# Hybrid attention/mLSTM layer: adaLN modulation by pairs of feature tiles, two last-gate tiles computed at the start, gate columns on head 0's token units

## The chip, the cores and the metric

One core of a Trainium2 chip. The metric is the device time of one execution in microseconds (us), the median of several runs. TensorE multiplies, VectorE (DVE), ScalarE (ACT) and GpSimd (POOL) do the elementwise work, SyncE (SP) and ScalarE issue the DMAs.

## What is computed

One layer on x of 1024 tokens by 1024 features, float32, cut here to what matters:

```python
mod = silu(c) @ w_ada + b_ada
shift, scale, gate = split(mod, 3)
h = rmsnorm(x, norm_w) * (1 + scale) + shift
proj = h @ w_in
aq, ak, av, az, mq, mk, mv, mo, mz, mi, mf, ga, gm = split(proj)
att = sliding_window_attention(rope(aq), rope(ak), av, sinks)   # 16 heads, 4 kv heads, window 128
y_att = (att * silu(az)) @ w_att_branch
hm = mlstm(silu(conv(mq)), silu(conv(mk)), mv, mi + b_i, log_sigmoid(mf + b_f))
y_m = (headnorm(hm) * sigmoid(mo) * silu(mz)) @ w_m_branch
merged = sigmoid(ga) * y_att + sigmoid(gm) * y_m
out = rmsnorm(x + gate * (merged @ w_out), final_norm_w)
```

w_ada has 1024 rows and 3072 columns: shift, scale, gate. w_in has 11,272 columns; mi and mf, the mLSTM's input and forget gates, are 4 columns each; gm, the last gate, is 1024 columns.

## The kernel before, in words

All operands of a large product are split into a high and a low part of 32 bits each (fp32r). A product is three matmuls (`passes`, lines 527 to 529): high x high, low x high, high x low. Features are cut into KT = 8 tiles of 128, tokens into NB = 8 blocks of 128 and two halves of 512.

Weights go through five slots of 128 columns. SP loads a slot (`raw`, 512 KB), POOL splits it with two instructions, w_hi (L482) and w_lo (L484), and TensorE uses it; who reads the last product of a slot frees it (`slot_free`). SP's, POOL's and TensorE's use of the slots is a written order: the tables SLOT_USES and BANK_USES say how often each phase uses a slot and a bank, and every wait is a count worked out from them. POOL takes the splits in program order and waits for a slot even where a later one is ready.

The start: x is loaded (4 MB), squared on ScalarE (L801), its row factors made on POOL (L469, L471), normalised on VectorE (L1040), turned on TensorE (L568) and copied to `xnt` by ScalarE (L806). The small vectors come behind x in SP's queue (L366 to L371). w_ada's shift and scale columns come row tile by row tile, 1 MB each; VectorE adds each, times silu(c), to `mod_acc` (L1083, L1086), and between them makes the rotation angles (L1056 to L1074). TensorE turns the sums (L575), VectorE adds up and makes scale and shift (L1092 to L1098). Then, tile by tile, ScalarE writes h_hi (L815), ScalarE or VectorE x_mod (L817, L1106), VectorE h_lo (L1115). Behind each h_lo, TensorE adds to the gate units: slot 4 holds the 8 columns of mi and mf in 128 mostly empty ones, two units of 512 tokens.

The phases after that: A (four kv heads; per head 8 token units of 384 columns for q, k and v, and 4 feature units for az, with rope, softmax and the attention products beside them; head 0 alone also carries the mLSTM's gate rows, `gate_row_step`), B (the attention branch), C (the mLSTM), D1 (sigmoid of the last gate gm, 8 feature tiles x 2 halves into `sig_m`; beside it ScalarE loads and VectorE sums w_ada's gate columns, L985, L1421), D2 (the mLSTM branch; before it ScalarE writes y_hi, L997, and VectorE y_lo, L1430) and E (w_out, residual, last norm). D1 and D2 use slots 0, 1, 2 and 4 in turn, twice each:

```python
for phase in ("D1", "D2"):
    with pool.Fori(0, 2, 1) as i:
        for s in D_SLOTS:
            split(s, use(phase, s, 0) + i, loads(phase, s, 1) + i)
```

Of the kernel before, what the change touches and what calls it, by code (L numbers as in the profile page):

```python
# [21 lines left out]
F32 = mybir.dt.float32  # L22
# [7 lines left out]
P = 128  # L30
# [30 lines left out]
SLOT_USES = {"G": (0, 0, 0, 0, 1), "A": (4,) * 5, "B": (4, 4, 4, 4, 0), "C": (8,) * 5,  # L61
             "D1": (2, 2, 2, 0, 2), "D2": (2, 2, 2, 0, 2), "E": (1, 1, 1, 1, 0), "E2": (1, 1, 1, 1, 0)}
SLOT_DMAS = {"G": (0, 0, 0, 0, 2), "A": (4, 4, 8, 4, 4), "B": (4, 4, 4, 4, 0), "C": (8,) * 5,
             "D1": (2, 2, 2, 0, 2), "D2": (2, 2, 2, 0, 2), "E": (1, 1, 1, 1, 0), "E2": (1, 1, 1, 1, 0)}
D_SLOTS = (0, 1, 2, 4)
BANK_USES = {"A": 24, "B": 16, "C": 48, "D1": 8, "D2": 8, "E": 8}
# [21 lines left out]
MOD_BY_ACT = (1, 4, 7)  # L88
# [6 lines left out]
def build(nc, x, c, positions, w_ada, b_ada, norm_w, w_in, b_if, att_sinks, conv_q, conv_k,  # L95
          m_norm_w, w_att, w_m, w_out, final_norm_w, inv_freq, out, row_pack, merged_dram):
    with ExitStack() as ctx:
# [29 lines left out]
        bias_if = sb("bias_if", [36, 1])  # L127
        scale1 = sb("scale1", [P, KT])
# [35 lines left out]
        def place(name, shape, dt, offset):  # L164
# [17 lines left out]
        w_mod = place("w_mod", [P, KT, 2 * D], F32, HT)  # L182
# [9 lines left out]
        mod_acc = place("mod_acc", [P, 2 * D], F32, X + 3072)  # L192
# [44 lines left out]
        gate_row = place("gate_row", [P, D], F32, RAW + 3 * 4096)  # L237
# [7 lines left out]
        w2_hi = place("w2_hi", [P, 4, KT, P], F32R, HT)  # L245
        w2_lo = place("w2_lo", [P, 4, KT, P], F32R, HT + 4 * 4096)
# [15 lines left out]
        mod_loaded = [sem(f"mod_loaded{n}") for n in range(KT + 1)]  # L262
# [91 lines left out]
        out_v = out.rearrange("(n p) d -> p n d", p=P)  # L354
        merged_v = merged_dram.rearrange("(k p) t -> p k t", p=P)
# [5 lines left out]
        def _(sp):  # L361
            for n in range(4):
                sp.dma_start(x_in[:, 2 * n:2 * n + 2, :], x_v[:, 2 * n:2 * n + 2, :]).then_inc(x_loaded[n], 16)
            for rows, v, n in ((V_C, c, 8), (V_NW, norm_w, 8), (V_SH, b_ada[0:D], 8), (V_SC, b_ada[D:2 * D], 8),
                               (V_CQ, conv_q, 32), (V_CK, conv_k, 32), (V_MN, m_norm_w, 8)):
                sp.dma_start(vec_rows[rows:rows + n, :], v.rearrange("(r p) -> r p", p=P)).then_inc(vec_loaded, 16)  # L366
            sp.dma_start(pos_i[:, :], positions.rearrange("(n p) -> n p", p=P)).then_inc(small_loaded, 16)
            sp.dma_start(freq[:, :], inv_freq[None, :].broadcast_to([P, HD // 2])).then_inc(small_loaded, 16)
            sp.dma_start(sink[:, :], att_sinks[None, :].broadcast_to([P, 16])).then_inc(small_loaded, 16)
            for q in range(2):  # L370
                sp.dma_start(bias_if[32 * q:32 * q + 4, :], b_if[4 * q:4 * q + 4, None]).then_inc(small_loaded, 16)  # L371

            sp.wait_ge(gate_slot_zeroed, 1)
            sp.dma_start(raw[:, 4, :, 0:4], w_in_v[:, :, MI:MI + 4]).then_inc(slot_loaded[4], 16)
            sp.dma_start(raw[:, 4, :, 32:36], w_in_v[:, :, MF:MF + 4]).then_inc(slot_loaded[4], 16)
            for k in range(KT - 1):
                sp.dma_start(w_mod[:, k, :], w_ada_v[:, k, 0:2 * D]).then_inc(mod_loaded[k], 16)
            for half in range(2):
                t = slice(half * D, (half + 1) * D)
                sp.dma_start(w_mod[:, KT - 1, t], w_ada_v[:, KT - 1, t]).then_inc(mod_loaded[KT - 1 + half], 16)  # L380

            def load(src, s, uses):
                after(sp, slot_split[s], uses)
                sp.dma_start(raw[:, s, :, :], src).then_inc(slot_loaded[s], 16)

            with sp.Fori(0, KVH, 1) as i:
# [6 lines left out]
                sp.dma_start(raw[:, 2, :, 0:HD], src_k).then_inc(slot_loaded[2], 16)  # L393
                sp.dma_start(raw[:, 2, :, HD:P], src_v).then_inc(slot_loaded[2], 16)
# [24 lines left out]
            with sp.Fori(0, 2, 1) as i:  # L419
                for k, s in enumerate(D_SLOTS):  # L420
                    src = w_in_v[:, :, bass.ds(sp.snap(GM + k * P + i * 512), P)]
                    load(src, s, use("D1", s, 0) + i)
# [1092 lines left out]
```

## Time and profile before

| what | value |
|---|---|
| runs | 1435.89, 1434.66, 1434.6 us; median 1434.66 |
| profiled execution, span | 1435.3 us (the listed runs lie around it; nothing else is listed for it) |
| TensorE busy | 1340.0 us (93%), 6846 matmuls |
| VectorE busy | 750.4 us (52%) |
| ScalarE, POOL busy | 396.6 us (28%), 491.6 us (34%) |
| mean DMA rate | 62 GB/s, 89.28 MB |

In the rows further down, PE is TensorE's matmuls, PEld its weight loads, DVE VectorE, ACT ScalarE, POOL GpSimd, SPq SyncE's queue. L527 is line 527 of the kernel. A matmul's duration is longer than the step from one to the next, since they are pipelined. PEclk is the granted clock of TensorE: 1.00 is 2.4 GHz, 0.50 is 1.2 GHz.

### The profile page before, as it was taken

Reading aid. Unit: us, or ns where it says so; the run is one execution under the profiler, and the core shown is the slowest. Engines: PE = TensorE matmul, PEld = TensorE weight load, DVE = VectorE, ACT = ScalarE, POOL = GpSimd, SP = SyncE. Lnnn points to the kernel's source line nnn. Section 1 sums busy time; section 2 is a strip of 40 time slices with the busy share of each in tenths; the row PEclk is TensorE's granted clock in tenths of the full one; section 3 lists DMA queues with packets and bytes.
Section 4 is the critical chain, followed back from the end, with each engine's and each line's share of the span. In section 5 each row is a group of like instructions: output and inputs, shape, how many; then the busy total and the mean of one; then the engine's idle time right before and its main releaser. Section 6 shows DMA issues by size and latency. Waiting matters only on the chain.

```text
span 1435.3 us, 19403 instructions
## 1 busy us (share of the span) xinstructions
PE 1340.0 (93%) x6846; PEld 1138.8 (79%) x6846; DVE 750.4 (52%) x1297; ACT 396.6 (28%) x926; POOL 491.6 (34%) x248
## 2 busy tenths in 40 slices
PE   2399998999989999999999999999999999899998
PEld 2297796978867888877988898889789888788886
DVE  5979888695776000065256426633672421366445
ACT  5342634334342010013221322233223311311111
POOL 4613204132045343273054205412531333335230
PEclk9599999999999999999999999999999999999999
DMA  9501102011021121050041004101310123322502
GB/s 350 137 15 30 45 2 59 15 29 29 0 58 35 54 88 59 15 162 16 1 117 44 0 0 132 29 0 41 91 44 15 44 74 98 107 76 68 193 16 103
DMA packets 119830, 89.28 MB, mean 62 GB/s; under 512 B 13305, under 2 KB 111721, under 8 KB 118894
## 3 DMA queue, kind: packets, MB, share of 16 engines
q1 hardware_dynamic: 116288, 76.16, 17.8%
q10 hardware_dynamic: 3502, 12.61, 2.5%
q8 instruction: 23, 0.38, 0.1%
q14 instruction: 17, 0.14, 0.0%
HBM read 80.35 MB, written 8.41 MB: 62 GB/s over the span
## 4 chain that ended last, share of the span: by engine, by line
PE 78%; DVE 14%; issue 4%; ACT 2%; DMA 1%; POOL 1%; DVEq 0%; ACTq 0%; SPq 0%; POOLq 0%
PE pp L527 22%; PE pp L529 22%; PE pp L528 22%; DVE conv L1382 2%; PE pp L713 2%; PE pp L723 2%; PE pp L633 1%; DVE prob L1232 1%; DVE y_lo L1289 1%; PE pp L624 1%; PE pp L602 1%; PE pp L616 1%; PE pp L705 1%; PE pp L617 1%; PE pp L718 1%
## 5 line engine op out<-in xcount | busy, mean ns | idle before, releaser
L482 POOL TENSOR_TENSOR w_hi<-raw,ones 128x1024 fp32r<-128x1024 f32 x101 | 201.4, 1994 | 828.6 <-ACTq L346 492.0
L527 PE MATMUL pp<-h_hi,w_hi 128*128 128x512 f32 x912 | 363.1, 398 | 14.8 <-DVE h_lo L1115 9.5
L528 PE MATMUL pp<-h_lo,w_hi 128*128 128x512 f32 x912 | 357.6, 392 | 0.0
L529 PE MATMUL pp<-h_hi,w_lo 128*128 128x512 f32 x912 | 357.1, 392 | 0.0
L484 POOL TENSOR_TENSOR w_lo<-raw,w_hi 128x1024 fp32r<-128x1024 f32 x101 | 257.2, 2546 | 7.9
L527 PEld LDWEIGHTS pp<-h_hi,w_hi 128*128 128x128 f32 x912 | 172.9, 190 | 52.6 <-issue 10.3
L529 PEld LDWEIGHTS pp<-h_hi,w_lo 128*128 128x128 f32 x912 | 172.6, 189 | 36.7
L528 PEld LDWEIGHTS pp<-h_lo,w_hi 128*128 128x128 f32 x912 | 172.9, 190 | 35.2
L527 PE MATMUL pp<-w_hi,h_hi 128*128 128x384 f32 (+1 forms) x512 | 162.1, 317 | 0.6 <-DVE roped L1209 0.6
L529 PE MATMUL pp<-w_hi,h_lo 128*128 128x384 f32 (+1 forms) x512 | 158.2, 309 | 0.0
L528 PE MATMUL pp<-w_lo,h_hi 128*128 128x384 f32 (+1 forms) x512 | 158.0, 309 | 0.0
L527 PE MATMUL pp<-y_hi,w_hi 128*128 128x512 f32 x256 | 101.7, 397 | 6.5 <-DVE y_lo L1430 4.2
L529 PE MATMUL pp<-y_hi,w_lo 128*128 128x512 f32 x256 | 101.2, 395 | 0.0
L528 PE MATMUL pp<-y_lo,w_hi 128*128 128x512 f32 x256 | 101.1, 395 | 0.0
L527 PEld LDWEIGHTS pp<-w_hi,h_hi 128*128 128x128 f32 x512 | 96.9, 189 | 3.2 <-issue 1.2
L528 PEld LDWEIGHTS pp<-w_lo,h_hi 128*128 128x128 f32 x512 | 97.0, 189 | 1.0
L529 PEld LDWEIGHTS pp<-w_hi,h_lo 128*128 128x128 f32 x512 | 96.9, 189 | 0.0
L1310 DVE TENSOR_TENSOR mix_a<-sig_a,pp 128x512 f32<-128x512 f32 x16 | 11.0, 687 | 144.3 <-PE pp L529 144.0
L1326 DVE SCALAR_TENSOR_TENSOR s_dec<-pp,dec 128x128 f32<-128x128 f32 x32 | 9.3, 292 | 136.3 <-PE pp L705 124.7
L527 PEld LDWEIGHTS pp<-y_hi,w_hi 128*128 128x128 f32 x256 | 48.9, 191 | 18.7 <-issue 3.2
L528 PEld LDWEIGHTS pp<-y_lo,w_hi 128*128 128x128 f32 x256 | 49.1, 192 | 10.2
L529 PEld LDWEIGHTS pp<-y_hi,w_lo 128*128 128x128 f32 x256 | 49.0, 191 | 10.3
(216 smaller groups left out, 1947.6 us busy)
## 6 DMA issues: line engine op xcount, KB each, us to landing
raw<-w_in SPq DMA_DIRECT2D x72, 512.0 KB, 3.8
w_mod<-w_ada SPq DMA_DIRECT2D x7, 1024.0 KB, 11.1
x_in<-x SPq DMA_DIRECT2D x4, 1024.0 KB, 8.2
raw<-w_att SPq DMA_DIRECT2D x8, 512.0 KB, 5.1
merged_dram<-mix_a ACTq DMA_DIRECT2D x8, 512.0 KB, 2.6
w_gate<-w_ada ACTq DMA_DIRECT2D x8, 512.0 KB, 3.5
raw<-w_m SPq DMA_DIRECT2D x8, 512.0 KB, 3.7
mix_in<-merged_dram ACTq DMA_DIRECT2D x8, 512.0 KB, 3.3
```

The lines of the kernel that those rows point to most:

```text
L482: pool.tensor_tensor(hi, raw[:, s, :, :], one, ALU.mult).then_inc(slot_hi[s], 1)
L484: pool.tensor_tensor(lo, raw[:, s, :, :], hi.bitcast(F32), ALU.subtract).then_inc(slot_split[s], 1)
L527: pe.matmul(o, lh, rh, start=first, stop=False)
L528: pe.matmul(o, lh, rl, start=False, stop=False)
L529: return pe.matmul(o, ll, rh, start=False, stop=last)
L602: ins = pe.matmul(bank(2)[:, g * P:(g + 1) * P], q_parts[:, m % 2, g, :, :], ident_r[:, :], start=True, stop=True)
L616: pe.matmul(o, q, k_hi[:, keys], start=True, stop=False)
L617: ins = pe.matmul(o, q, k_lo[:, keys], start=False, stop=True)
L624: ins = pe.transpose(bank(5)[:, g * P:(g + 1) * P], prob[:, g, :], ident[:, :])
L713: ins = pe.matmul(bank(4)[:, 0:MV], mq_t[:, f, n * P:(n + 1) * P], state[:, f, :], start=(f == 0), stop=(f == 1))
L723: ins = pe.matmul(bank(6 + f)[:, 0:MV], k_w[:, n % 2, f * P:(f + 1) * P], v_aug[:, n % 2, :], start=True, stop=True)
L1382: dve.scalar_tensor_tensor(out=conv[:, :], in0=xpad[:, j:j + S], scalar=taps[:, j, n // 2:n // 2 + 1], in1=conv[:, :], op0=ALU.mult, op1=A ...
```

## The change

Four things change together.

1. **w_ada by pairs of feature tiles.** SP loads it in four pairs (2 MB each: 256 shift and 256 scale columns, all 1024 rows, in rows of 1 KB). Of a pair's 8 row tiles VectorE sums 4 (pair 0) or 6 (pairs 1 to 3) into `mod_acc`, TensorE takes the other 4 or 2 as one-column matmuls straight from w_mod and adds VectorE's sum by a matmul with ones (`mod_sums`). Scale and shift of a pair are ready by themselves, and h follows by pairs. The rotation angles come after the last h_lo.
2. **Two of the eight tiles of D1 at the start.** w_in's columns of gm tiles 0 and 1 are loaded first of all into slots 3 and 4 and split by ScalarE and VectorE. Behind each h_lo, TensorE runs 12 matmuls: two tiles, two halves, three passes. ScalarE takes the sigmoids, stores them to DRAM (`early_dram`) and loads them back before D1. D1 has six tiles left.
3. **Gate columns on head 0.** The weight store is laid out as 8 + 5 x 128 columns per row tile, and the 8 columns of mi and mf stand ahead of slot 0, so that head 0's token units take 392 columns instead of 384. VectorE copies the 8 columns of each block to `g_tok`; TensorE turns them at the start of head 1, and they go through DRAM (`gate_dram`) to rows. `gate_row_step` runs in head 1.
4. The small loads are issued by ScalarE; POOL makes the row factors of x by twos.

The diff, cut to its core:

```diff
-SLOT_USES = {"G": (0, 0, 0, 0, 1), "A": (4,) * 5, "B": (4, 4, 4, 4, 0), "C": (8,) * 5,
-             "D1": (2, 2, 2, 0, 2), "D2": (2, 2, 2, 0, 2), "E": (1, 1, 1, 1, 0), "E2": (1, 1, 1, 1, 0)}
+SLOT_USES = {"G": (0, 0, 0, 1, 1), "A": (4,) * 5, "B": (4, 4, 4, 4, 0), "C": (8,) * 5,
+             "D1": (2, 2, 1, 0, 1), "D2": (2, 2, 2, 0, 2), "E": (1, 1, 1, 1, 0), "E2": (1, 1, 1, 1, 0)}
+EARLY = 2
+D1_TILES = [(tile, D_SLOTS[n % 4], n // 4) for n, tile in enumerate(range(EARLY, KT))]
+GATE_LOADS = (2, 2, 1, 1, 1, 1)
+PAIRS = KT // 2
+J_PE = (4, 2, 2, 2)
+SUMS_BEFORE = (0, 0, 2, 4)
+WCOLS = G8 + 5 * P
...
         def _(sp):
+            for n in range(EARLY):
+                sp.dma_start(raw[:, :, cols_of(3 + n)], w_in_v[:, :, GM + n * P:GM + (n + 1) * P]).then_inc(slot_loaded[3 + n], 16)
...
-            for k in range(KT - 1):
-                sp.dma_start(w_mod[:, k, :], w_ada_v[:, k, 0:2 * D]).then_inc(mod_loaded[k], 16)
+            for p in range(PAIRS):
+                for half in range(2):
+                    src = w_ada_v[:, :, half * D + 2 * P * p:half * D + 2 * P * (p + 1)]
+                    sp.dma_start(w_mod[:, half, p, :, :], src).then_inc(mod_loaded[p], 16)
+            sp.dma_start(raw[:, :, 0:G8], w_in_v[:, :, MI:MI + G8]).then_inc(g8_loaded, 16)
...
-            for phase in ("D1", "D2"):
-                with pool.Fori(0, 2, 1) as i:
-                    for s in D_SLOTS:
-                        split(s, use(phase, s, 0) + i, loads(phase, s, 1) + i)
+            for _, s, n in D1_TILES:
+                split(s, use("D1", s, n), loads("D1", s, n + 1))
+            with pool.Fori(0, 2, 1) as i:
+                for s in D_SLOTS:
+                    split(s, use("D2", s, 0) + i, loads("D2", s, 1) + i)
...
+            def mod_sums(p):
+                pe.wait_ge(mod_loaded[p], 32)
...
+                for j in range(KT - J_PE[p], KT):
+                    for half in range(2):
+                        for kk in range(2):
+                            pe.matmul(bank((0, 6)[half] + kk)[:, p:p + 1], w_mod[:, half, p, j, kk * P:(kk + 1) * P], silu_c[:, j:j + 1],
+                                      start=(j == KT - J_PE[p]), stop=False)
+                pe.wait_ge(mod_summed, sum(KT - J_PE[m] for m in range(p + 1)))
...
             pe.wait_ge(x_evac, 16)
...
             for k in range(KT):
+                for p in range(PAIRS):
+                    if SUMS_BEFORE[p] == k:
+                        mod_sums(p)
                 pe.wait_ge(h_lo_ready, k + 1)
...
+                for n in range(2 * EARLY):
+                    s, half = 3 + n // 2, n % 2
...
         def _(act):
+            for s in (3, 4):
+                act.wait_ge(slot_loaded[s], 16)
+                act.activation(w_hi[:, :, cols_of(s)], raw[:, :, cols_of(s)], ACT.Copy).then_inc(slot_hi[s], 1)
+            act.wait_ge(vecs_ready, 1)
+            act.activation(silu_c[:, :], vecs[:, V_C:V_C + KT], ACT.Silu).then_inc(silu_c_ready, 1)
...
         def _(dve):
+            mod_products(0)
+            mod_scale(0)
+            mod_products(1)
+            split_h(0)
+            mod_scale(1)
+            split_h(1)
+            mod_products(2)
+            split_h(2)
+            mod_scale(2)
+            split_h(3)
+            mod_products(3)
+            split_h(4)
+            mod_scale(3)
+            for k in range(5, KT):
+                split_h(k)
...
             attend(0)
-            with dve.Fori(0, KVH - 1, 1) as i:
+            attend(1, 0, gate_rows=True)
+            with dve.Fori(1, KVH - 1, 1) as i:
                 attend(i + 1, i)
```

How instructions move, at three places.

VectorE at the start, from the first sum over w_ada on, before (a part; `mod_acc` is the running sum, `ang` and `turns` the angles):

```order
L1083 TENSOR_SCALAR mod_acc<-w_mod,silu_c 128x2048 [waits mod_loaded0,silu_c_ready,angle_step]
L1056 TENSOR_TENSOR ang<-pos_col,freq 128x256
L1086 SCALAR_TENSOR_TENSOR mod_acc<-w_mod,silu_c,mod_acc 128x2048 [waits mod_summed,mod_loaded1]
L1060 TENSOR_SCALAR turns<-ang 128x256 [waits angle_step]
L1086 SCALAR_TENSOR_TENSOR mod_acc<-w_mod,silu_c,mod_acc 128x2048 [waits mod_summed,mod_loaded2]
```

and now:

```order
L1168 TENSOR_SCALAR mod_acc<-w_mod,silu_c 128x512 [waits silu_c_ready,mod_loaded0]
L1171 SCALAR_TENSOR_TENSOR mod_acc<-w_mod,silu_c,mod_acc 128x512 [waits mod_summed] x3
L1179 TENSOR_TENSOR scale_t<-pp,sc_bias 128x2 [waits vecs_ready,mod_full]
L1180 TENSOR_TENSOR shift<-pp,vecs 128x2
L1182 TENSOR_TENSOR scale<-scale_t,vecs 128x2 [waits mod_step]
L1168 TENSOR_SCALAR mod_acc<-w_mod,silu_c 128x512 [waits silu_c_ready,mod_loaded1]
L1171 SCALAR_TENSOR_TENSOR mod_acc<-w_mod,silu_c,mod_acc 128x512 [waits mod_summed] x5
L1196 TENSOR_TENSOR h_lo<-x_mod,h_hi 128x1024 [waits h_hi_ready,x_mod_act]
```

The sums are short and dependent, each pair's scale stands behind its own sum, and the angles are gone from between them.

ScalarE at its beginning, before:

```order
L801 ACT_TABLE_LOAD
L801 ACTIVATE pp,x_ssq<-x_in 128x1024 [waits x_loaded0]
L801 ACTIVATE pp,x_ssq<-x_in 128x1024 [waits x_squared,x_loaded0]
```

and now:

```order
L840 DMA pos_i<-positions 8x128
L841 DMA freq<-inv_freq 128x32
L842 DMA sink<-att_sinks 128x16
L844 DMA bias_if<-b_if 4x1 x2
L848 ACT_TABLE_LOAD
L848 ACTIVATE w_hi<-raw 128x8x128 [waits slot_loaded3]
L848 ACTIVATE w_hi<-raw 128x8x128 [waits slot_loaded4]
L850 ACT_TABLE_LOAD
L850 ACTIVATE silu_c<-vecs 128x8 [waits vecs_ready]
L857 ACTIVATE pp,x_ssq<-x_in 128x1024 [waits x_loaded0]
```

The loads, the two splits and silu now stand ahead of the squares.

POOL at the end of D1 and the beginning of D2, before (the body of the loop over D2, behind the same body for D1, which ends with slot 4):

```order
L481 REGISTER_ALU [waits slot_free0]
L482 TENSOR_TENSOR w_hi<-raw,ones 128x1024 [waits slot_loaded0]
L112 REGISTER_ALU
L484 TENSOR_TENSOR w_lo<-raw,w_hi 128x1024 [waits slot_hi0]
L482 TENSOR_TENSOR w_hi<-raw,ones 128x1024 [waits slot_loaded1,slot_free1]
L484 TENSOR_TENSOR w_lo<-raw,w_hi 128x1024 [waits slot_hi1]
L481 ISA [waits slot_free2]
L482 TENSOR_TENSOR w_hi<-raw,ones 128x1024 [waits slot_loaded2]
```

and now the last four rows of D1, which ends with slots 0 and 1 (slot 4 stands just ahead of them), and the first of D2's loop:

```order
L496 TENSOR_TENSOR w_hi<-raw,ones 128x8x128 [waits slot_loaded0,slot_free0]
L498 TENSOR_TENSOR w_lo<-raw,w_hi 128x8x128 [waits slot_hi0]
L496 TENSOR_TENSOR w_hi<-raw,ones 128x8x128 [waits slot_loaded1,slot_free1]
L498 TENSOR_TENSOR w_lo<-raw,w_hi 128x8x128 [waits slot_hi1]
L525 UNCONDITIONAL_BRANCH
L525 ISA
L495 REGISTER_ALU [waits slot_free0]
L496 TENSOR_TENSOR w_hi<-raw,ones 128x8x128 [waits slot_loaded0]
```

D2's slot order is as before, 0, 1, 2, 4, but the tiles of D1 that free them last are now in slots 0 and 1, and were in slots 2 and 4.

## Rows read from the trace of the kernel before

**Rows 1.** The page: the chain that ended last, shares of the span by engine.
```profile
PE 78%; DVE 14%; issue 4%; ACT 2%; DMA 1%; POOL 1%; DVEq 0%; ACTq 0%; SPq 0%; POOLq 0%
```
**Rows 2.** By stretch: length; PE, PEld, DVE, ACT, POOL busy; PEclk; DMA share, GB/s.
```profile
60.00:70.00 10.00, 5.19 (x12) 4.14 (x13) 9.08 (x11) 7.84 (x7) 1.83 (x1) 0.50 0.32 81
```
**Rows 3.** The chain in order of time, start and us: the scale.
```profile
61.96 0.18 DVE scale L1098
```
**Rows 4.** By stretch, stage D1.
```profile
1158.20:1245.30 87.10, 87.10 (x385) 71.82 (x383) 18.60 (x15) 9.59 (x16) 35.44 (x16) 1.00 0.33 97
```
**Rows 5.** Timeline of TensorE (start, us, engine, line): gate units, first of head 0.
```profile
66.22 0.63 PE L527 MATMUL pp<-h_hi,w_hi 128*128 128x512 f32 x1
66.65 0.63 PE L528 MATMUL pp<-h_lo,w_hi 128*128 128x512 f32 x1
...
78.70 0.33 PE L527 MATMUL pp<-w_hi,h_hi 128*128 128x384 f32 x1
78.87 0.34 PE L528 MATMUL pp<-w_lo,h_hi 128*128 128x384 f32 x1
```
**Rows 6.** Timeline, the small loads on SP, and their first reader.
```profile
2.98 0.42 SPq L366 DMA_DIRECT2D vec_rows<-c  x1
...
6.90 0.67 SPq L371 DMA_DIRECT2D bias_if<-b_if  x2
...
15.31 0.41 PE L556 MATMUL pp<-ident,vec_rows 104*128 104x104 f32 x1 [15.31 <-DMA vec_rows<-m_norm_w]
```
**Rows 7.** Timeline of ScalarE at the start: table load, squares, evacuations.
```profile
0.81 1.28 ACT L801 ACT_TABLE_LOAD   x1 [0.81 <-PEq L1485]
...
7.01 1.03 ACT L801 ACTIVATE pp<-x_in 128x1024 f32<-128x1024 f32 x1
...
8.26 1.03 ACT L801 ACTIVATE pp<-x_in 128x1024 f32<-128x1024 f32 x1
...
29.94 6.53 ACT L806 ACTIVATE xnt<-pp 128x512 f32<-128x512 f32 x13 [0.25 <-PE pp L568]
```
**Rows 8.** Timeline 33 to 73 us, VectorE, POOL and TensorE's turns of mod_acc.
```profile
33.04 2.34 DVE L1086 SCALAR_TENSOR_TENSOR mod_acc<-w_mod,silu_c,mod_acc 128x2048 f32<-128x2048 f32 x1
...
38.57 3.96 POOL L482 TENSOR_TENSOR w_hi<-raw,ones 128x1024 fp32r<-128x1024 f32 x1 [12.67 <-DMA raw<-w_in]
...
40.70 3.98 DVE L1086 SCALAR_TENSOR_TENSOR mod_acc<-w_mod,silu_c,mod_acc 128x2048 f32<-128x2048 f32 x1
42.61 4.27 POOL L484 TENSOR_TENSOR w_lo<-raw,w_hi 128x1024 fp32r<-128x1024 f32 x1
...
50.13 1.94 PE L575 MATMUL pp<-ident,mod_acc 128*128 128x128 f32 x8 [14.88 <-DVE mod_acc L1086]
...
71.77 0.81 DVE L1106 TENSOR_SCALAR x_mod<-xnt,scale,shift 128x1024 f32<-128x1024 f32 x1
...
72.49 3.58 DVE L1115 TENSOR_TENSOR h_lo<-x_mod,h_hi 128x1024 fp32r<-128x1024 f32 x3
```
**Rows 9.** Timeline from D1 to D2: POOL, VectorE, TensorE.
```profile
1236.65 2.40 POOL L484 TENSOR_TENSOR w_lo<-raw,w_hi 128x1024 fp32r<-128x1024 f32 x1
1245.55 1.89 POOL L482 TENSOR_TENSOR w_hi<-raw,ones 128x1024 fp32r<-128x1024 f32 x1 [6.50 <-ACTq L346]
1247.52 2.70 POOL L484 TENSOR_TENSOR w_lo<-raw,w_hi 128x1024 fp32r<-128x1024 f32 x1
...
1246.68 12.51 DVE L1430 TENSOR_TENSOR y_lo<-y,y_hi 128x512 fp32r<-128x512 f32 x16 [5.24 <-ACT y_hi L997]
...
1250.82 0.80 PE L527 MATMUL pp<-y_hi,w_hi 128*128 128x512 f32 x1 [1.43 <-DVE y_lo L1430]
```
**Rows 10.** Timeline of VectorE: the first rope product of heads 0, 1 and 2.
```profile
84.81 0.49 DVE L1201 TENSOR_TENSOR rot_c<-pp,cos 128x320 f32<-128x320 f32 x1
...
173.06 0.48 DVE L1201 TENSOR_TENSOR rot_c<-pp,cos 128x320 f32<-128x320 f32 x1
...
260.05 0.48 DVE L1201 TENSOR_TENSOR rot_c<-pp,cos 128x320 f32<-128x320 f32 x1
```

More of the change, by code:

```diff
@@ L417, in _ @@
                         sp.dma_start(dec[:, :], src).then_inc(dec_loaded, 16)
[L419 to L422, printed above, removed]
+            for tile, s, n in D1_TILES:
+                load(w_in_v[:, :, GM + tile * P:GM + (tile + 1) * P], s, use("D1", s, n))
             with sp.Fori(0, 2, 1) as i:
@@ L581, in _ @@
+            pe.wait_ge(x_evac, 16)
             for k in range(KT):
+                for p in range(PAIRS):
+                    if SUMS_BEFORE[p] == k:
+                        mod_sums(p)
                 pe.wait_ge(h_lo_ready, k + 1)
-                for half in range(2):
+                for n in range(2 * EARLY):
+                    s, half = 3 + n // 2, n % 2
+                    if k == 0 and half == 0:
+                        after(pe, slot_split[s], use("G", s, 1))
                     t = slice(half * HALF, (half + 1) * HALF)
-                    ins = passes(bank(6 + half), (w_hi[:, 4, k, :], w_lo[:, 4, k, :]), (h_hi[:, k, t], h_lo[:, k, t]),
-                                 k, k == 0, k == KT - 1)
@@ L587, in _ @@
-            ins.then_inc(gates_full, 1)
+                    ins = passes(bank(2 + n), (w_hi[:, k, cols_of(s)], w_lo[:, k, cols_of(s)]),
+                                 (h_hi[:, k, t], h_lo[:, k, t]), k, k == 0, k == KT - 1)
+                    if k == KT - 1:
+                        ins.then_inc(early_full, 1)
             def turn_k(i, m):
@@ L753, in _ @@
                             ins.then_inc(h_turned, 1)
-            for phase, hi, lo, ready in (("D1", h_hi, h_lo, None), ("D2", y2_hi, y_lo, y2_lo_ready)):
-                with pe.Fori(0, 2, 1) as i:
-                    for k, s in enumerate(D_SLOTS):
-                        after(pe, slot_split[s], use(phase, s, 1) + i)
-                        for half in range(2):
-                            feature_unit(phase, 4, i, 2 * k + half, s, half, hi, lo, ready=ready)
+            for e, (_, s, n) in enumerate(D1_TILES):
+                after(pe, slot_split[s], use("D1", s, n + 1))
+                for half in range(2):
+                    feature_unit("D1", 0, 0, 2 * e + half, s, half, h_hi, h_lo)
+            with pe.Fori(0, 2, 1) as i:
+                for k, s in enumerate(D_SLOTS):
+                    after(pe, slot_split[s], use("D2", s, 1) + i)
+                    for half in range(2):
+                        feature_unit("D2", 4, i, 2 * k + half, s, half, y2_hi, y_lo, ready=y2_lo_ready)
             pe.wait_ge(gate_bias_added, 1)
@@ L773, in _ @@
                         after(pe, slot_split[s], use("E2", s, 1))
-                wh, wl = (w_hi[:, 0:4], w_lo[:, 0:4]) if half == 0 else (w2_hi[:, :], w2_lo[:, :])
                 for n in range(NB):
@@ new lines, in split_h @@
+            def split_h(k):
+                by_act = sum(m in MOD_BY_ACT for m in range(k + 1))
+                if k in MOD_BY_ACT:
+                    dve.wait_ge(x_mod_act, by_act)
+                else:
+                    dve.wait_ge(mod_step, 4 * (k // 2 + 1))
+                    dve.wait_ge(x_evac, 16)
+                    dve.tensor_scalar(x_mod[:, k, :], xnt[:, k, :], scale1[:, k:k + 1], shift[:, k:k + 1],
+                                      ALU.mult, ALU.add).then_inc(x_mod_dve, 1)
+                    dve.wait_ge(x_mod_dve, k + 1 - by_act)
+                dve.wait_ge(h_hi_ready, k + 1)
+                dve.tensor_tensor(h_lo[:, k, :], x_mod[:, k, :], h_hi[:, k, :].bitcast(F32), ALU.subtract).then_inc(h_lo_ready, 1)
```

369 lines of the change are left out of this document (205 added, 164 removed).

## The prediction

> **What bounds the kernel now.** I read first who carries the chain that ended last: TensorE 78% of the span, VectorE 14% [rows 1]. So a microsecond of matmul removed where TensorE runs without a gap is a microsecond gained; work moved to where TensorE waits can be free. The table by stretch shows such a place: from 60 to 70 us TensorE is busy 5.19 of 10 us at a granted clock of 0.50 [rows 2]. The chain says why: the modulation scale is ready at 61.96 us [rows 3], after all 8 MB of w_ada have been summed on VectorE; no matmul with weights can start before. The other end of the change, the last-gate stage D1, is the opposite: 87.10 us without an idle moment, clock 1.00 [rows 4]. Its 384 matmuls (8 tiles x 2 halves x 8 k x 3) give 0.2268 us each.
>
> **Part 1: two of eight D1 tiles go to the start.** D1 loses 96 matmuls x 0.2268 = **-21.8 us**, all on the path [rows 4]. Its weight splits, its eight w_gate loads and sums keep their number; they fit, since VectorE is busy only 18.60 of the 87 us.
>
> **Part 2: the start.** Before, head 0's first matmul is at 78.70 us [rows 5]; I work out when it comes now.
> ScalarE: it now issues the twelve small loads, which took SP 2.98 to 7.57 = 4.6 us [rows 6], so it is free at 5.4. Then a table load 1.28, two copies of 128x1024 at about 1.25, a table load 1.28, silu 0.21: 10.7. Eight squares at a pitch of 1.25: 20.7 [rows 7] (x stands behind 1 MB of w_in now, but is there before ScalarE gets to it). Sixteen evacuations at 0.60 (13 in 6.53 before, less what overlaps; [rows 7]): 30.3.
> TensorE then makes 20 one-column products of w_ada. The nearest row is the eight 128x128 transposes of mod_acc, 1.94 us at half clock, so 0.24 each there and 0.12 at full clock [rows 8]; I take 0.12, as the transposes of x have just ended: 2.4 us. Three tiny vector operations: 0.6. **First scale at 33.4**, against 61.96. The bound above is 0.24, +2.4 us more; below, nothing.
> VectorE from there, in its written order: three times six products of 512 columns. 2048 columns take 2.34, so 512 cost some 0.62, and with the wait for their own result 0.8; the first is a plain multiply, 0.5: 4.5 x 3 = 13.5. Eight h_lo at 1.19 (3 in 3.58) = 9.5, four x_mod at 0.81 = 3.2 [rows 8], three scale triples at 0.6 = 1.8, about 1.5 of waits for TensorE and ScalarE: 29.5, so **62.9** if nothing disturbs it.
> POOL disturbs it. In the same stretch before, VectorE's 2.34 us sum takes 3.98 and POOL's 2.40 us w_lo takes 4.27 [rows 8]: the first ends at 44.68, the second at 46.88, each having waited for the whole instruction of the other. They alternate. The Trainium skill, SBUF — State Buffer, section "Who interferes with whom", calls this an exclusive lock between the two, held for a whole instruction; the trace agrees, with 3.98 for 2.34. Head 0's first slot was split from 38.57 us [rows 8], as soon as it had landed behind w_ada; behind 1 MB more of SP's loads that is some 41 us. Slots 0, 1 and 2 are split then by six POOL instructions, 3 x (1.89 + 2.40) = 12.9 us (durations of [rows 9], before any wait). New is that h_lo and the products lie in just this stretch, with a gap after each in which POOL comes in. Taken in full: last h_lo at **75.8**. Slots 3 and 4 wait for the early units.
> Behind the last h_lo lie twelve matmuls: 2.7 us at full clock, 12 x 0.43 = 5.1 at the low one [rows 5]. I take 4.2: **head 0 starts at 80.0, +1.3**. Its third token unit needs bank 0 back, so the first rope. That now waits for four sigmoids, a store, a table load, sin, and cos on VectorE, while POOL splits slots 3 and 4 (8.6 us): about +1.2 more than the 8 us of two units hide. Together **+2.5**. Bounds: with POOL's 12.9 hidden, -10.5; with the low clock in all 96 early matmuls (41 us behind the first h_lo at 39.5, and the sums) and dear products, +7.
>
> **Part 3: gate columns on head 0.** The 48 gate matmuls at the start are replaced by 8 columns in 192 matmuls. 384 columns step by 0.173 and 512 by 0.2268, so 8 columns cost 3.3 ns: **+0.6** [rows 4, 5].
>
> **Part 4: D1 to D2.** POOL splits slots in the written order. Before, when D1 ended only slot 4 was left: w_hi at 1245.55 and w_lo at 1247.52; the second y_lo, and with it TensorE's second matmul group at 1250.82, waited for that [rows 9]. Now the last tiles use slots 0 and 1, and slots 2 and 4, long free, stand behind slot 1 in POOL's queue. So three splits instead of one fall on the sixteen y_lo (12.51 us, [rows 9]): four more POOL instructions, 2 x 4.3 = 8.6 us, before the sixth y_lo. TensorE had hidden about 2.5 us of y_lo behind its low clock there; it gets that clock for longer and loses it again. **+8**; bounds 0 (VectorE goes first) and +10.
>
> **Part 5: the heads.** Row steps move from head 0 to head 1, and the gate rows go through DRAM. First rope to first rope is 88.25 us in head 0 and 86.99 in head 1 [rows 10], so these steps cost little more than 1.3 where they stand. Eight copies of 8 columns, two more table loads and a DRAM trip in a busier head: **+1**, bounds -2 and +4. The strided layout of w_hi and w_lo I cost at nothing: DMA rows stay 512 bytes, and POOL is idle between splits; if each split took longer, it would show in parts 2 and 4.
>
> **Sum** against the profiled execution's span: 1435.3 - 21.8 + 2.5 + 0.6 + 8 + 1 = 1425.6. The span lies 0.6 above the median of 1434.66, so **1425.0**. Low ends: 1435.3 - 21.8 - 10.5 + 0.6 + 0 - 2 = 1401.6; high ends: 1435.3 - 21.8 + 7 + 0.6 + 10 + 4 = 1435.1.
>
> **Rivals.**
> A. *POOL hardly hurts.* Its instructions fall into VectorE's waits (x_evac, the sums) and VectorE goes first at D2. Then part 2 gives up to -10.5 and part 4 nothing: 1403 to 1414, say **1408**. Against it: in [rows 8] POOL came in after every VectorE operation.
> B. *The low clock.* TensorE waits between its bursts of twelve, and after its wait at the start it worked at the low clock [rows 2, 5]. If each burst runs at 1.2 GHz, the early units end at 83 to 84 and D2 begins slower: **1431**. The Trainium skill, TensorE: Matmul & The Clock Gate, section "HAM oscillation — how this bites in real kernels", holds that bursts broken by waits each start at the low clock, which speaks against feeding TensorE tile by tile; by it the time would be this rival's.
> C. *Gate rows stall head 1.* ScalarE waits for a store and VectorE for two loads, and table loads stand before the softmax; if none of it is covered, two trips of about 3 us and 2 x 1.28 us: **1434**.
> D. *Slower: the vectors land late.* Silu stands ahead of the squares on ScalarE and needs the seventh vector load, which landed at 15.3 us before, behind 4 MB of x [rows 6]. On ScalarE's own queue I expect 6 to 8. If it comes only behind all 13 MB of SP's queue, near 39 us, the squares start 30 us late; POOL's 12.9 are then hidden: +17, **1442**. It starts to cost at 10 us and eats the gain by about 20.
>
> **How the numbers follow.** The sum 0.56; A 0.16; B 0.10, of which 0.04 within 0.2%; C 0.10, of which 0.06 within and 0.04 above; D 0.08. 0.2% is 2.9 us, about what a measurement can tell from no change. Faster 0.56 + 0.16 + 0.06 = 0.78; same 0.10; slower 0.12. The range takes in the sum's bounds, most of A, B and part of C: 1407 to 1434.
>
> **What would show it.** First scale near 33 us; w_hi and w_lo of slots 0 to 2 between the products, each VectorE operation beside them 2 us long; head 0's first matmul near 80; D1 in 65.3 us without a gap; after it six POOL instructions in a row, and y_lo some 20 us long for sixteen. I am wrong if head 0 starts before 72 or after 87, if D1 has gaps, or if y_lo takes 13 us as before.

## The result, and the profile after

The changed kernel takes 1446.90 us (median of 4 runs, 1445.56 to 1448.26) against 1434.63 for the kernel before: ratio 1.0077, 95% interval 1.0064 to 1.0089. It is **slower by 12.3 us**; the forecast was 1425.0, with 1434 as its upper end. The profiled execution took 1445.56 us with a span of 1443.8.

What the forecast named at the start came true within 2 us. The start, in the timelines of TensorE, VectorE and POOL of the changed kernel (start, length, engine, line, output<-inputs):

```profile
28.29 3.76 PE L595 MATMUL pp<-silu_c,w_mod 128*128 128x1 f32 x32 [1.30 <-ACT xnt L860]
...
34.12 0.16 DVE L1182 TENSOR_TENSOR scale<-scale_t,vecs 128x2 f32<-128x2 f32 x1
```
```profile
43.55 12.42 DVE L1171 SCALAR_TENSOR_TENSOR mod_acc<-w_mod,silu_c,mod_acc 128x512 f32<-128x512 f32 x5
55.90 3.36 DVE L1196 TENSOR_TENSOR h_lo<-x_mod,h_hi 128x1024 fp32r<-128x1024 f32 x1
...
74.17 1.22 DVE L1196 TENSOR_TENSOR h_lo<-x_mod,h_hi 128x1024 fp32r<-128x1024 f32 x1
```
```profile
43.39 1.89 POOL L496 TENSOR_TENSOR w_hi<-raw,ones 128x1024 fp32r<-128x1024 f32 x1 [21.91 <-DMA raw<-w_in]
45.36 2.72 POOL L498 TENSOR_TENSOR w_lo<-raw,w_hi 128x1024 fp32r<-128x1024 f32 x1
```

The scale comes at 34.1 (forecast 33.4; [rows 3] had 61.96), in part by luck, as the account of part 2 below shows. POOL's six split instructions, of which two are shown, lie from 43.4 to 58.2, and in that stretch five products that take 3.90 us elsewhere take 12.42. The last h_lo ends at 75.4 (forecast 75.8). Head 0's first matmul comes at 81.78 (forecast 80.0; [rows 5] had 78.70).

The turn from D1 to D2, timelines of POOL and VectorE; it answers to [rows 9]:

```profile
1243.64 1.89 POOL L496 TENSOR_TENSOR w_hi<-raw,ones 128x1024 fp32r<-128x1024 f32 x1 [6.64 <-ACTq L369]
1245.61 2.70 POOL L498 TENSOR_TENSOR w_lo<-raw,w_hi 128x1024 fp32r<-128x1024 f32 x1
1248.27 2.34 POOL L496 TENSOR_TENSOR w_hi<-raw,ones 128x1024 fp32r<-128x1024 f32 x1
...
1255.76 2.68 POOL L498 TENSOR_TENSOR w_lo<-raw,w_hi 128x1024 fp32r<-128x1024 f32 x1
```
```profile
1244.78 20.23 DVE L1535 TENSOR_TENSOR y_lo<-y,y_hi 128x512 fp32r<-128x512 f32 x16 [5.39 <-ACT y_hi L1074]
```

Six POOL instructions in a row, sixteen y_lo in 20.2 us instead of 12.5: as forecast. And the chain is of the same make as in [rows 1]:

```profile
PE 76%; DVE 15%; ACT 4%; issue 4%; DMA 1%; DVEq 0%; SPq 0%; ACTq 0%
```

So the time went elsewhere. I set the same events of the two traces side by side; each line is the length of one stretch:

| stretch | before | after | difference | forecast |
|---|---|---|---|---|
| start to the first rope of head 0 | 84.8 | 90.0 | +5.2 | +2.5 |
| head 0, first rope to first rope | 88.3 | 86.0 | -2.2 | gates +0.6, and the row steps' share of +1 |
| head 1 | 87.0 | 95.1 | +8.1 | the rest of that +1 |
| head 2 | 86.4 | 86.9 | +0.5 | 0 |
| head 3, stages B and C, to the first sigmoid of D1 | 818.3 | 825.8 | **+7.4** | 0 |
| D1, first to last sigmoid | 80.7 | 59.8 | -20.9 | -21.8 |
| last sigmoid of D1 to first merged | 13.6 | 21.3 | +7.7 | +8 |
| D2, E and the stores | 176.2 | 178.9 | **+2.7** | 0 |

Sum +8.5, the difference of the spans. The other 3.8 of the 12.3 lie between executions: every execution that is listed with its span has a time 1.7 to 1.8 above it, so the profiled one of before stands for some 1437.1, 2.4 above the median of its kernel, and the profiled one of the changed kernel lies 1.3 below its median (its four runs are two and two, 1445.6 and 1445.9, 1447.9 and 1448.3; the last section comes back to that).

Two things are large and were not in the sum: head 1, and a slow drift through stages that the diff hardly touches. The drift is in the step from matmul to matmul. Stretches of TensorE in D1, in E's first half and in E's second half (length, busy with count, clock, DMA share, GB/s), kernel before:

```profile
1190.00:1230.00 40.00, 40.00 (x179) 1.00 0.32 95
1375.00:1390.00 15.00, 15.00 (x68) 1.00 0.00 0
1412.00:1427.00 15.00, 15.00 (x68) 1.00 0.25 102
```

The same stretches of the changed kernel:

```profile
1190.00:1230.00 40.00, 40.00 (x175) 1.00 0.40 119
1375.00:1390.00 15.00, 15.00 (x66) 1.00 0.01 2
1412.00:1427.00 15.00, 15.00 (x68) 1.00 0.25 103
```

No idle time and the clock at 2.4 GHz in both, but fewer matmuls in the same 40 us. The start times of the matmuls in D1 give a step of 0.2267 us before and **0.2314** after, and so do all 512-column units of B, C and D2 with w as their weights; 0.2325 in E's first half, where w is the moving operand; and again 0.2267 in E's second half, whose w2 tiles are laid out apart.

### The profile page after: what moved, and what is told of

Read it like the earlier page. It is cut to its first block, busy times and chain, and to the rows that moved or that the text cites. A ratio compares the mean times of both kernels' runs of the same rounds, so it can differ in the third digit from the quotient of the medians.

```text
span 1443.8 us, 19335 instructions
## 1 busy us (share of the span) xinstructions
PE 1365.1 (95%) x6895; PEld 1147.0 (79%) x6895; DVE 756.7 (52%) x1327; ACT 402.2 (28%) x932; POOL 471.3 (33%) x234
## 4 chain that ended last, share of the span: by engine, by line
PE 76%; DVE 15%; ACT 4%; issue 4%; DMA 1%; DVEq 0%; SPq 0%; ACTq 0%
PE pp L541 21%; PE pp L543 21%; PE pp L542 21%; DVE conv L1487 2%; PE pp L752 2%; PE pp L762 2%; DVE prob L1336 2%; PE pp L663 1%; DVE y_lo L1394 1%; PE pp L654 1%; PE pp L744 1%; PE pp L646 1%; DVE mod_acc L1171 1%; PE pp L632 1%; PE pp L647 1%
## 5 line engine op out<-in xcount | busy, mean ns | idle before, releaser
L496 POOL TENSOR_TENSOR w_hi<-raw,ones 128x1024 fp32r<-128x1024 f32 x98 | 194.9, 1989 | 849.6 <-ACTq L369 516.8
L498 POOL TENSOR_TENSOR w_lo<-raw,w_hi 128x1024 fp32r<-128x1024 f32 x98 | 249.3, 2544 | 7.7
L542 PEld LDWEIGHTS pp<-h_lo,w_hi 128*128 128x128 f32 x896 | 170.0, 190 | 38.7
L541 PE MATMUL pp<-w_hi,h_hi 128*128 128x256 f32 (+2 forms) x512 | 163.0, 318 | 1.4 <-DVE roped L1313 1.3
L542 PE MATMUL pp<-w_lo,h_hi 128*128 128x256 f32 (+2 forms) x512 | 158.4, 309 | 0.0
L543 PE MATMUL pp<-w_hi,h_lo 128*128 128x256 f32 (+2 forms) x512 | 158.4, 309 | 0.0
```

The source lines that it names most:

```text
L496: pool.tensor_tensor(hi, raw[:, :, cols_of(s)], one, ALU.mult).then_inc(slot_hi[s], 1)
L498: pool.tensor_tensor(lo, raw[:, :, cols_of(s)], hi.bitcast(F32), ALU.subtract).then_inc(slot_split[s], 1)
L541: pe.matmul(o, lh, rh, start=first, stop=False)
L542: pe.matmul(o, lh, rl, start=False, stop=False)
L543: return pe.matmul(o, ll, rh, start=False, stop=last)
```

## The experiments

### Where a matmul's operand starts

The changed layout puts eight gate columns ahead of the slots in each row of w_hi and w_lo: a slot starts 32 bytes into a row, and rows are 2592 bytes apart, so that seven of the eight rows of a slot start 32 to 224 bytes past a multiple of 256. (Starts are counted from the kernel's base address here and below. The source rounds the base up to a multiple of 64; no run shows where it lies beyond that.) I first took the start alone, in the kernel before:

```diff
-        WHI, WLO = RAW + 5 * 4096, RAW + 10 * 4096
-        YO = WLO + 5 * 4096
+        WHI, WLO = RAW + 5 * 4096 + 32, RAW + 10 * 4096 + 32
+        YO = WLO + 5 * 4096 + 32
```

> The kernel before, with w_hi and w_lo each moved by 32 bytes (and what lies behind them by 64), nothing else. Theory 1: a stationary operand that starts at 32 bytes past a multiple of 64 costs each matmul 4.5 ns (the 512-column pitch of the feature units was 0.2267 us in the kernel before and 0.2312 in the changed one, and stayed 0.2267 in stage E, where w is the moving operand). Then the pitch in D1 becomes 0.2312 here, and 3504 such matmuls give +15.8: about 1450. Theory 2: it is the row pitch of 2592 bytes, or the strided write, or the unrolled code, that costs it: then the pitch stays 0.2267 and the time 1434.7.

Measured: 1453.47 us, ratio 1.0126 (1.0108 to 1.0144), the kernel before on the same chip at 1436.88. D1 shows the fewest matmuls yet:

```profile
1190.00:1230.00 40.00, 40.00 (x173) 1.00 0.32 95
```

The step is 0.2333, and +16.6 us for a shift of 32 bytes (64 for what lies behind w_lo). In D1 the moving operand h has not moved, so the step there is the doing of the weights' start alone: theory 1, though with 6.6 ns and not 4.5, and the row pitch is not needed for it. My aside on stage E in that expectation was wrong: it holds for E's second half only. Here that half steps by 0.2333 too; its weights g_hi have moved by 64 bytes, g_lo and w2 have not.

In the changed kernel, eight more unused columns (G8 = 8 is the number of gate columns):

```diff
+OFF = 2 * G8
-WCOLS = G8 + 5 * P
+WCOLS = OFF + 5 * P
-            return slice(G8 + s * P, G8 + (s + n) * P)
+            return slice(OFF + s * P, OFF + (s + n) * P)
```

> The changed kernel with eight unused columns ahead of the gate columns, so that the slots start at 64 bytes and the row pitch is 2624. Theory 1 (alignment of the stationary operand): the 512-column pitch of the feature units is 0.2267 again, 3456 matmuls x 4.5 ns less: 1446.9 - 15.5 = 1431. Theory 2 (the row pitch or the strided write as such): pitch 0.2312, time 1446.9.

Measured: 1448.84 us, ratio 1.0077 (1.0060 to 1.0095), step 0.2317. **A miss**: rows that start at 64, 128, 192 and 0 bytes past a multiple of 256 in turn gain nothing. That did not clear the alignment, only my 64. Two more shifts of the kernel before:

```diff
-        WHI, WLO = RAW + 5 * 4096, RAW + 10 * 4096
-        YO = WLO + 5 * 4096
+        WHI, WLO = RAW + 5 * 4096 + 128, RAW + 10 * 4096 + 128
+        YO = RAW + 15 * 4096 + 256
```

> The kernel before with w_hi and w_lo each moved by 128 bytes (what lies behind w_lo by 256), nothing else. With 32 bytes the 512-column pitch of every unit with w as stationary operand was 0.2333 us instead of 0.2267. Theory 1 (only multiples of 256 bytes are free of the cost): pitch 0.2333 in D1 again, time + some 14 to 16. Theory 2 (a multiple of 128 is enough): 0.2267, time as before.

Measured: 1453.24 us (2 runs), ratio 1.0117 (1.0088 to 1.0146); step 0.2323 in D1 and where w moves in E's first half, and 0.2267 in E's second half. Theory 1, with a step a little shorter than expected.

```profile
1190.00:1230.00 40.00, 40.00 (x174) 1.00 0.32 92
```

The same with 256 in place of 128 on the first line:

> The kernel before with w_hi and w_lo each moved by 256 bytes. Theory 1 (a multiple of 256 is enough, as for g_hi, which stands at 256 past a multiple of 512 in the changed kernel and steps by 0.2267): pitch 0.2267, time as before. Theory 2 (512 is needed, or the distance between the two operands counts): pitch above 0.2267, time + 10 or more.

Measured: 1437.06 us, ratio 1.0003 (0.9992 to 1.0014), step 0.2267.

```profile
1190.00:1230.00 40.00, 40.00 (x178) 1.00 0.36 105
```

So of the shifts of w tried (32, 128 and 256 bytes) only 256 is free; 64 was seen only mixed with others, in a_off64's rows, and in g_hi. Then the cure in the changed kernel: raw stays as it is, w_hi and w_lo get rows of 704 columns.

```diff
 WCOLS = G8 + 5 * P
+OFF = 64
+WPAD = OFF + 5 * P
-        w_hi = place("w_hi", [P, KT, WCOLS], F32R, WHI)
-        w_lo = place("w_lo", [P, KT, WCOLS], F32R, WLO)
+        w_hi = place("w_hi", [P, KT, WPAD], F32R, WHI)
+        w_lo = place("w_lo", [P, KT, WPAD], F32R, WLO)
```

> The changed kernel with w_hi and w_lo padded to rows of 704 columns, slots from column 64, so that each stationary operand starts at a multiple of 256 bytes; raw keeps its rows of 648. Theory 1 (start of the stationary operand): pitch 0.2267 in all feature units, B, C, D1, D2 give back some 10 to 12: 1435 to 1437. Theory 2 (the row pitch that is no multiple of the slot, or reading and writing with a stride): pitch stays 0.2312, time 1446.9.

Measured: 1437.41 us, ratio **0.9998** (0.9985 to 1.0010): the whole loss is gone. Step 0.2267 throughout:

```profile
1190.00:1230.00 40.00, 40.00 (x178) 1.00 0.35 100
```

Against the table above, head 3 to D1 is +0.3 instead of +7.4, D1 58.4 instead of 59.8, and D2 to the end -0.2 instead of +2.7: 11.4 us of layout. It still reads and writes with a stride that is no multiple of a slot (2816 bytes, a slot being 512) and keeps the odd raw rows, so theory 2 is out. By count it could have been more: 3456 matmuls x 4.7 ns = 16.2. The 1536 of stage C gave back 2.5 of their 7.2 (first to last s_dec 464.1 us before the cure, 461.6 with it); what else bounds that stage was not looked into.

### The turn from D1 to D2

```diff
-D1_TILES = [(tile, D_SLOTS[n % 4], n // 4) for n, tile in enumerate(range(EARLY, KT))]
+D1_TILES = [(2, 0, 0), (3, 1, 0), (4, 2, 0), (5, 4, 0), (6, 2, 1), (7, 4, 1)]
```

(and D1's slot uses and loads (1, 1, 2, 0, 2).)

> The changed kernel with D1's six tiles in slots 0, 1, 2, 4, 2, 4 instead of 0, 1, 2, 4, 0, 1. Theory 1 (POOL's queue at the turn from D1 to D2 costs about 8 us): only slot 4 is left to split when D1 ends, the sixteen y_lo take 12.5 us instead of 20, and the time is 1446.9 - 7.5 = 1439.4. Theory 2 (TensorE's low clock or y_lo itself sets the turn): below 2 us gained, 1445 or above.

Measured: 1441.05 us, ratio 1.0029 (1.0014 to 1.0044), 6 to 7 below the changed kernel. POOL and VectorE there:

```profile
1247.01 1.89 POOL L496 TENSOR_TENSOR w_hi<-raw,ones 128x1024 fp32r<-128x1024 f32 x1 [3.02 <-ACTq L369]
1248.98 2.70 POOL L498 TENSOR_TENSOR w_lo<-raw,w_hi 128x1024 fp32r<-128x1024 f32 x1
```
```profile
1248.07 12.59 DVE L1535 TENSOR_TENSOR y_lo<-y,y_hi 128x512 fp32r<-128x512 f32 x16 [3.00 <-ACT y_hi L1074]
```

One split instead of three, y_lo in 12.6, last sigmoid to first merged 13.7 instead of 21.3. Theory 1: part 4 was right in mechanism and size.

### The gate rows in head 1

ScalarE in head 1 of the changed kernel, and VectorE's fourth and fifth rope there:

```profile
197.60 1.06 ACT L899 ACTIVATE row_e<-row_e 4x1024 f32<-4x1024 f32 x1
198.68 1.28 ACT L901 ACT_TABLE_LOAD   x1
199.97 1.06 ACT L901 ACTIVATE row_e<-row_e 4x1024 f32<-4x1024 f32 x1
201.05 0.60 ACT L924 ACTIVATE q_t<-pp 128x512 fp32r<-128x512 f32 x1
201.55 0.27 ACT L925 ACTIVATE k_hi<-pp 128x128 fp32r<-128x128 f32 x1
201.84 1.28 ACT L931 ACT_TABLE_LOAD   x1
```
```profile
195.42 0.48 DVE L1305 TENSOR_TENSOR rot_c<-pp,cos 128x320 f32<-128x320 f32 x1
...
201.85 0.29 DVE L1326 TENSOR_TENSOR k_lo<-pp,k_hi 128x128 fp32r<-128x128 f32 x1 [2.96 <-ACT k_hi L925]
...
206.10 0.48 DVE L1305 TENSOR_TENSOR rot_c<-pp,cos 128x320 f32<-128x320 f32 x1
```

Exp, a table load, Ln and the table load back are 4.7 us, and the softmax of the block stands behind them: 10.7 us from rope to rope, 6.5 in the kernel before. Before, these two stood in step 0 of head 0, where no softmax runs yet. Moved to where ScalarE waited 11.4 us:

```diff
-                if n == 4:
-                    act.wait_ge(row_step, 5)
...
                     if 4 <= u <= NB + 3:
                         exponentials(i, u - 4)
+                    if gate_rows and u == 8:
+                        act.wait_ge(row_step, 5)
...
```

> The changed kernel with ScalarE's Exp and Ln of the gate rows in head 1 moved from the end of step 4 to step 8, where ScalarE waited 11.4 us for the last rope. Theory 1 (these two and the two table loads around them, 4.7 us, stand in the path of the softmax): the fifth rope of head 1 comes 6.5 us after the fourth instead of 10.7, and the time is about 4 us less, 1443. Theory 2 (head 1 is limited by VectorE, which has the row steps on top): 1446 to 1447, the 4 us come back by the eighth rope.

Measured: 1441.12 us, ratio 1.0035 (1.0021 to 1.0048). Fourth to fifth rope is 6.5 again:

```profile
195.99 0.48 DVE L1304 TENSOR_TENSOR rot_c<-pp,cos 128x320 f32<-128x320 f32 x1
...
202.47 0.48 DVE L1304 TENSOR_TENSOR rot_c<-pp,cos 128x320 f32<-128x320 f32 x1
```

Head 1 takes 90.1 us instead of 95.1. Theory 1, a little stronger than expected. The 3 us still above the other heads stand beside the row steps that VectorE has on top there; they were not taken apart.

### All three

> The changed kernel with the 256-byte rows, D1 in slots 0, 1, 2, 4, 2, 4, and Exp and Ln of the gate rows at step 8 of head 1. If the three costs are separate places of one path, the gains add: 1446.9 - 11 - 6 - 5 = 1425, below the kernel before by 10. If one is hidden behind another, 1428 to 1435.

Measured: **1423.76 us**, ratio 0.9914 (0.9891 to 0.9936), the kernel before at 1437.03. From the changed kernel's 1.0077 that is -0.0163; the three single ratios give -0.0079, -0.0048 and -0.0042, together -0.0169. Within these intervals they add, as three places on one path would.

### The start

POOL held back until h_lo is made:

```diff
+            pool.wait_ge(h_lo_ready, KT)
             with pool.Fori(0, KVH, 1) as i:
                 for s in range(5):
```

> The kernel of a_three, with POOL's first split held back until all eight h_lo are made. Theory 1 (my step in part 2: six POOL instructions take 12.9 us out of VectorE's row of products and h_lo): the last h_lo ends near 63 us instead of 77, slots 0 to 2 are split from then on and head 0's first matmul comes near 77 instead of 83, 4 to 6 us less: 1418 to 1420. Theory 2 (POOL's work falls into waits of VectorE that are there anyway): the last h_lo comes at most 3 us earlier and head 0 starts 10 us later: 1433.

Measured: 1421.93 us, ratio 0.9903 (0.9886 to 0.9919). The last h_lo starts at 64.8 instead of 74.5:

```profile
54.64 3.90 DVE L1179 SCALAR_TENSOR_TENSOR mod_acc<-w_mod,silu_c,mod_acc 128x512 f32<-128x512 f32 x5
...
64.81 1.23 DVE L1204 TENSOR_TENSOR h_lo<-x_mod,h_hi 128x1024 fp32r<-128x1024 f32 x1
```

POOL's 12.9 us did cost VectorE 9.7. But head 0 starts at 79.8 instead of 82.0, the first rope comes at 89.0 instead of 90.3, and by head 1 nothing is left (175.4 against 175.0). The mechanism is theory 1's; the gain is neither theory's, and within the interval it is none. TensorE is through with the early units at 72.5 there and stands idle until head 0, which needs slots 0 to 2; the last of POOL's six split instructions for them, now behind the h_lo, ends at 79.6:

```profile
79.79 0.66 PE L549 MATMUL pp<-w_hi,h_hi 128*128 128x392 f32 x1 [7.26 <-issue]
```

So the splits hold head 0 back there. The Trainium skill, SBUF — State Buffer, section "Who interferes with whom", says that VectorE and GpSimd hold their shared port pair exclusively; the trace agrees, with the same five products at 12.42 us beside POOL and 3.90 without.

A second candidate for what ate the rest: sin and cos. In the changed kernel they come late, and cos runs beside POOL's split of slot 4 (85.12 to 89.53):

```profile
83.13 1.28 ACT L882 ACT_TABLE_LOAD   x1 [0.47 <-ACT sig_early L878]
84.43 0.42 ACT L882 ACTIVATE sin<-ang 128x256 f32<-128x256 f32 x1
```
```profile
85.26 2.04 DVE L1221 TENSOR_TENSOR turns<-turns 128x256 f32<-128x256 f32 x1 [6.03 <-ACT turns L883]
87.33 2.36 DVE L1223 TENSOR_SCALAR cos<-turns 128x256 f32<-128x256 f32 x1
...
90.01 0.48 DVE L1305 TENSOR_TENSOR rot_c<-pp,cos 128x320 f32<-128x320 f32 x1
```

```diff
+            act.wait_ge(angle_step, 9)
+            act.activation(sin[:, :, :], ang[:, :, :], ACT.Sin)
+            act.activation(turns[:, :, :], ang[:, :, :], ACT.Sin, scale=0.5).then_inc(half_sin, 1)
             for n in range(2 * EARLY):
                 act.wait_ge(early_full, n + 1)
```

(The same three lines are gone from behind the sigmoids.)

> The kernel of a_three, with ScalarE's two Sin ahead of the four sigmoids of the early units instead of behind them. Theory 1 (the first rope waits for sin and cos, which wait for the sigmoids and then for POOL's splits): cos is done before POOL splits slot 3, the first rope comes near 87 instead of 90.3, 3 us less: 1421. Theory 2 (head 0 is limited by VectorE or by POOL's splits of slots 3 and 4, and takes the 3 us back by the fourth rope): 1423 to 1424.

Measured: 1420.55 us, ratio 0.9886 (0.9870 to 0.9903). In its trace the first scale is 3 us later than in a_three's (37.3 against 34.2), and still the first rope comes earlier, at 89.1; to B's first y_lo it is 0.6 ahead in spite of those 3. That speaks for theory 1. But at head 1 it is 1.3 us behind a_three (176.2 against 175.0), the two intervals overlap, and the two profiled executions take the same time (1420.2 and 1419.9): a gain over a_three is not shown. Cos takes 0.29 now:

```profile
83.19 0.29 DVE L1230 TENSOR_SCALAR cos<-turns 128x256 f32<-128x256 f32 x1
```

Both together:

> The kernel of a_three with both: Sin ahead of the sigmoids, and POOL's first split behind the last h_lo. Theory 1 (the first rope was bounded by the cos chain, so that the earlier start of head 0 in t_pool, 79.8 against 82.0 us, could not be used): first rope near 84 to 85 and 1418. Theory 2 (head 0's second half is bounded elsewhere, by POOL's splits and VectorE, as t_pool's first ropes of head 1, 175.4 against 175.0, suggest): 1420 to 1421, no better than t_sin.

Measured: 1422.48 us, ratio 0.9900 (0.9883 to 0.9916). First rope at 87.3, but head 1's at 175.0, as in a_three. Theory 2: what head 0's beginning gains, head 0 takes back. What holds it there was not tested.

### Without the early tiles

> The kernel of a_three without early tiles: all eight D1 tiles in D1 (slots 0, 1, 2, 4 twice), modulation still by pairs. Theory 1 (the early tiles save D1's 21.8 us and cost 5 to 7 at the start, behind the last h_lo): 1423.8 + 21.8 - 6 = 1439 to 1441. Theory 2 (they cost next to nothing, since POOL's splits hold head 0 back anyway): 1445. Theory 3 (they cost half of what they save): 1433 to 1435.

Measured: 1444.16 us, ratio 1.0052 (1.0033 to 1.0071), 20 us above a_three. That is theory 2's number: with the early units the kernel gains 20 of D1's 21.8 us. It is a net figure and not the early units' own price, for two more things stand in its trace, which also begins 3 us late (first scale at 37.3). Without early units POOL finds slots 3 and 4 free and splits all five ahead of the last h_lo, which moves to 83.0. And TensorE, with little between its waits, stays at the low clock until head 0 is under way:

```profile
31.00:60.00 29.00, 14.92 (x68) 0.50 0.81 220
60.00:88.00 28.00, 10.66 (x42) 0.50 0.15 39
```

What the early units cost with POOL's order unchanged was not run.

## Why the prediction was wrong, by its own steps

- **Part 1** (-21.8): D1 got 20.9 shorter; 22.3 with the layout mended. Right.
- **Part 2** (+2.5): the first scale and the last h_lo came within 0.7 us of the forecast. For the scale that is luck: the evacuations ended at 28.2 instead of 30.3, and the one-column products, priced at 2.4 us, took 5.5 (28.29 to 33.76; each shows as two records). VectorE's row and POOL's part in it were right. From the last h_lo on I allowed 4.2 us for twelve matmuls; it took 6.4, because 27 were left. The last h_lo is not what held head 0: TensorE had waited for the third h_lo until 59.3,

```profile
59.32 0.79 PE L541 MATMUL pp<-h_hi,w_hi 128*128 128x512 f32 x1 [1.42 <-DVE h_lo L1196]
```

  and had no gap from there to head 0: 24 matmuls, the last sums, and from 69.1 on the other 48, the first nine of them at the low clock (columns as above):

```profile
69.00:73.00 4.00, 4.00 (x12) 0.57 0.00 0
73.00:82.00 9.00, 9.00 (x41) 1.00 0.00 0
```

  The first rope then came 8.2 us behind the first matmul, 6.1 in the kernel before: the two VectorE instructions of cos took 4.4 us beside POOL instead of the 0.7 of t_sin. The +1.2 named them and left out that slowing. Undersized by 2.7 in all, within its bounds.
- **Part 3** (+0.6): head 0 got 2.2 shorter, row steps gone and gate columns there. With all starts at multiples of 256 bytes, 392 columns step by 178.3 ns and 384 by 173.3: 1.0 us for 192 matmuls.
- **Part 4** (+8): +7.7. Right.
- **Part 5, rows** (+1, bounds -2 and +4): head 1 paid 8.1, and heads 0 and 1 together, without the gate columns' 1.0, 4.9. This step failed. I read 1.3 us off [rows 10] as what these steps cost "where they stand", and that reading was of a place without a softmax. Rival C had the mechanism (two table loads before the softmax), but put its price at two trips and 2 x 1.28. That is 8.6, near the 8.1 by luck: with the trips still there, a_expln's head 1 gave back 5.0 of the 8.1. Those 5.0 were Exp, Ln and their two table loads in ScalarE's order; the other 3 were not taken apart.
- **Part 5, layout** ("I cost at nothing"): this is **the largest step that failed**. I looked at the DMA rows and at POOL's splits and not at the engine that reads them in 3456 matmuls of 512 columns: 11.4 us of span. Without it the ratio is 0.9998, so it is what made the kernel slower; that no gain is left even then comes from the rows of part 5, the start's 2.7, smaller lines of the table and the spread between executions.
- **Low and high ends**: the 1435.1 left out a price for layout altogether, so 1434 held no room for it.
- **Rivals**: D (late vectors) did not happen, silu came at 10.4 us. A did not either. B's low clock was there in part, as the two lines above show.
- My list of what would show me wrong looked only at places that I had priced; nearly every item came out as forecast while the time was 21.9 us off; only D1 took 66.6 us instead of 65.3, the layout's share in it. A count of matmuls in equal stretches, in a stage that the change leaves alone, would have been the missing line.

## What to carry to other kernels

When a tile is re-laid so that something can ride along, keep every start of a matmul operand at a multiple of 256 bytes, counted as above; a few unused columns cost nothing here and the lack of them 11 us. Price a moved step by what is queued behind it at the new place, not by what it cost at the old one. And compare the step from instruction to instruction in stages that the change does not touch: a drift of 2% has no wait, no gap and no releaser to show it.

## What the runs showed that I had not expected

- A 512-column fp32 matmul at the full clock steps by 0.2267 us if both operands start at a multiple of 256 bytes; in D1 by 0.2333 with the weights 32 bytes off (b_off32) and by 0.2323 with 128 (b_off128); in E's first half by 0.2323 and 0.2325 with the moving operand off (b_off128 and the changed kernel), and by 0.2311 with w, which moves there, 32 bytes off and g_hi 64 (b_off32). The Trainium skill, SBUF — State Buffer, section "Operand start alignment", asks only for multiples of the element size and says that its runs timed nothing; the traces here show that what is legal is not free. With 384 columns, where w moves, the step is 173.3 ns in place and with 32 bytes off, 176.0 with 128; with 256 columns the changed kernel loses nothing (118.0 against 119.7). Only fp32 operands were seen; other offsets occur only mixed, row by row (0.2314 in steps of 32, 0.2317 in steps of 64).
- The start has two lengths. In some executions the granted clock falls from 1.00 to 0.50 early in the first 32 one-column records (at about 30.4 us in a_slots, which begins them at 29.1) and not near their end (31.9 in the changed kernel's own trace); they take 5.84 us instead of the 3.76 above, and the first scale comes at 37.0 instead of 34.1. This is the row in the trace of a_slots:

```profile
29.08 5.84 PE L595 MATMUL pp<-silu_c,w_mod 128*128 128x1 f32 x32 [1.17 <-ACT xnt L860]
```

The changed kernel's four runs stand about 2 us apart in two pairs, which fits; but only one of the four has a trace, and the kernel before, which has no such products, spreads as widely (1434.3 to 1439.8 in 19 runs), so it is not shown to be the cause.
